# Every fourth expert's value row summed by the vector engine into SBUF instead of by TensorE

## The reference, cut to what matters

```
act = gelu(einsum('btd,bthkd->bthk', xi, u_tab[expert]))            # 8 heads x 16 experts for each token
ffn = einsum('bthk,bthkd->btd', gate * act, v_tab[expert])
x   = layer_norm(4 ** 0.25 * x + ffn, ln2_g, ln2_b)                 # x: 256 tokens x 1024
```

## Time and profile before

| | |
|---|---|
| time, median of 3 runs (lowest to highest) | 2979.73 us (2973.87 to 2981.59) |
| the profiled execution's own time | 2973.29 us |
| its span, first to last instruction | 2971.5 us |
| TensorE busy | 2618.1 us, 88% |
| VectorE busy | 1431.6 us, 48% |
| ScalarE busy | 916.0 us, 31% |
| GpSimd busy | 681.0 us, 23% |
| expert rows moved by DMA | 536.90 MB of 839.09 MB |
| first expert fetch issued, last expert matmul ended | 1175.57 us, 2960.93 us |
| shares of the chain that ended last | PE 61%, DVE 15%, DMA 14%, ACT 7% |

### The profile page before, as it was taken

How to read it: one execution, slowest core, us unless ns; L and a number is a source line. 1 busy time by engine, 2 the same in 40 slices (tenths; PEclk the granted TensorE clock), 3 DMA queues, 4 the chain that set the end, 5 groups by cost and what they waited for, 6 DMA issues and landing times.

```text
span 2971.5 us, 30335 instructions
## 1 busy us (share of the span) xinstructions
PE 2618.1 (88%) x11408; PEld 1774.3 (60%) x11408; DVE 1431.6 (48%) x3191; ACT 916.0 (31%) x2318; POOL 681.0 (23%) x615
## 2 busy tenths in 40 slices
PE   7776999878999995999998899999799999878776
PEld 6665888755884884766554566565376655443222
DVE  3776333242001234665546654545665554676444
ACT  1452111220000120354523235432334442333333
POOL 0010111110000001223233323333322333433432
PEclk9888999998999997999999999999899999999999
DMA  6220211214332665998999898999999899998997
GB/s 253 85 78 38 77 66 43 71 57 156 142 142 107 262 242 213 395 394 359 365 418 419 347 389 356 421 411 419 388 359 400 337 383 416 408 378 332 419 421 329
DMA packets 109986, 839.09 MB, mean 282 GB/s; under 512 B 12176, under 2 KB 12432, under 8 KB 13968
## 3 DMA queue, kind: packets, MB, share of 16 engines
q0 software_dynamic: 73728, 536.90, 44.8%
q1 hardware_dynamic: 36112, 300.25, 25.6%
HBM read 836.06 MB, written 1.05 MB: 282 GB/s over the span
## 4 chain that ended last, share of the span: by engine, by line
PE 61%; DVE 15%; DMA 14%; ACT 7%; issue 2%; POOL 1%; SPq 0%; POOLq 0%; DVEq 0%; ACTq 0%
PE psm L2129 17%; DMA mem<-in_puv,mem 14%; PE psm L427 10%; PE psm L1701 6%; PE psm L435 5%; DVE mem L2173 3%; PE psm L1348 3%; PE psm L716 3%; PE psm L2004 3%; PE psm L1245 3%; PE psm L1891 2%; PE psm L1396 1%; DVE mem L672 1%; PE psm L431 1%; PE psm L731 1%
## 5 line engine op out<-in xcount | busy, mean ns | idle before, releaser
L2129 PE MATMUL psm<-mem 128*128 128x512 f32 x2048 | 1017.5, 625 | 164.7 <-ACT mem L2147 160.8
L2173 DVE CUSTOM_DVE_ANT_0 mem<-mem 128x1024 f32<-128x1024 f32 x512 | 624.4, 1223 | 466.8 <-DMA mem<-in_puv,mem 463.0
L2157 POOL DMA_INDIRECT mem<-in_puv,mem x512 | 563.4, 1100 | 1205.4 <-PE psm L2129 1146.0
L2129 PEld LDWEIGHTS psm<-mem 128*128 128x128 f32 x2048 | 376.0, 196 | 607.8 <-ACT mem L2147 300.5
L427 PE MATMUL psm<-mem 128*128 128x256 f32 (+2 forms) x1504 | 355.1, 400 | 55.7 <-DVE mem L534 36.0
L427 PEld LDWEIGHTS psm<-mem 128*128 128x128 f32 x1504 | 294.5, 198 | 115.5 <-issue 52.7
L2141 ACT ACTIVATE mem<-mem 128x1 f32<-128x1 f32 x512 | 102.3, 200 | 692.0 <-DVE mem L2173 688.9
L1701 PE MATMUL psm<-mem 128*128 128x256 f32 x1024 | 243.7, 385 | 0.5 <-ACT mem L1424 0.5
L1701 PEld LDWEIGHTS psm<-mem 128*128 128x128 f32 x1024 | 196.2, 193 | 68.8 <-issue 45.0
L2147 ACT ACTIVATE mem<-mem 128x128 f32<-128x128 f32 x512 | 206.0, 402 | 17.0 <-PE psm L2129 0.3
L435 PE MATMUL psm<-mem 128*128 128x128 f32 x1408 | 191.2, 280 | 19.4 <-ACT mem L984 5.9
(11 more groups left out here) (356 smaller groups left out, 2413.6 us busy)
## 6 DMA issues: line engine op xcount, KB each, us to landing
mem<-in_w2g SPq DMA_DIRECT2D x64, 1024.0 KB
mem<-in_w SPq DMA_DIRECT2D x18, 2048.0 KB, 8.4
mem<-in_pwq SPq DMA_DIRECT2D x32, 1024.0 KB
mem<-in_w2f SPq DMA_DIRECT2D x28, 1024.0 KB
mem<-in_wgu SPq DMA_DIRECT2D x11, 2048.0 KB, 7.5
mem<-in_w2t SPq DMA_DIRECT2D x20, 1024.0 KB
mem<-in_w2b SPq DMA_DIRECT2D x16, 1024.0 KB
mem<-in_w2o SPq DMA_DIRECT2D x16, 1024.0 KB
```

What stands on the lines that cost most here:

```text
L2129: m = pe.matmul(bank(6 + h), DG[:, n % 4, :], GR[n % PING][:, 1024 + h * 512:1536 + h * 512], start=k == 0, stop=k == 127)
L2157: po.indirect_dma_start(GR[n % PING], None, A[f"puv{i // 2}"], bass.IndirectOffsetOnAxis(ap=IX[i % 2][:, k:k + 1], axis=0)).then_inc(gsem[ ...
L2173: ve.tensor_tensor_reduce(out=GR[n % PING][:, 0:1024], in0=GR[n % PING][:, 0:1024], in1=X[:, i % 2, :], scale=1.0, scalar=0.0, op0=MUL, op ...
```

## The change

The steps with n % 4 == 1 (32 of each tile, 128 in all) are summed by VectorE: `add_v(n)` runs behind the dot product of step n + 2, waits for `EA[n]`, and adds the coefficient times the v half to `ACC`, 1024 numbers for each partition in SBUF, with one `scalar_tensor_tensor` (the first of a tile overwrites `ACC` with a `tensor_scalar`). ScalarE makes no diagonal matrix and TensorE no matmuls for them. The buffer of such a step is freed by VectorE's mark `ED[n]`. The other 384 steps go as before. Behind the last of a tile, k = 125, VectorE also adds 4 ** 0.25 times x to `ACC`. `fin_ve` then adds `ACC` to the PSUM banks with `tensor_tensor` where it had `scalar_tensor_tensor` with x.

```diff
--- before.py
+++ after.py
@@ -221,6 +221,7 @@
         GT_ = [at(place(128), 128) for t in range(2)]
         DO = [at(place(128), 128) for t in range(2)]
         CO = [at(place(128), 128) for t in range(2)]
+        ACC = at(place(1024), 1024)
         assert placed[0] <= NF
         KY = at(5 * 2048, 16, 128)
         QP = at(scr, 16, 128)
@@ -400,9 +401,15 @@
         TP = marks("t_p", [(i, c) for i in RI for c in R4])
         TA = marks("t_a", [(i, c, x) for i in RI for c in R4 for x in ("s", "e")])
         TV = marks("t_v", [(i, c, x) for i in RI for c in R4 for x in ("ix", "g3", "gt")])
-        EP, EA, EV = [marks(n, range(NE)) for n in ("e_p", "e_a", "e_v")]
+        by_dve = [n for n in range(NE) if n % 4 == 1]
+        by_pe = [n for n in range(NE) if n % 4 != 1]
+        EP, ED = marks("e_p", by_pe), marks("e_d", by_dve)
+        EA, EV = marks("e_a", range(NE)), marks("e_v", range(NE))
+
+        def taken(n):
+            return EP[n] if n in EP.value else ED[n]
         PP = marks("p_p", [(i, c) for i in R2 for c in R2])
-        PV = marks("p_v", [(i, x) for i in RI for x in ["x0", "x1", "st", "l"] + ["h"] * (i < 2)])
+        PV = marks("p_v", [(i, x) for i in RI for x in ["ac", "x0", "x1", "st", "l"] + ["h"] * (i < 2)])
         PA = marks("p_a", R2)
         PO = marks("p_o", RI)
 
@@ -2117,6 +2124,7 @@
 
 
 
+
         def expert_pe(pe):
             yield
             yield
@@ -2124,10 +2132,12 @@
                 i, k = n // 128, n % 128
                 if k == 0 and i:
                     pe.wait_ge(*PV[i - 1, "x1"])
-                pe.wait_ge(*EA[n])
-                for h in R2:
-                    m = pe.matmul(bank(6 + h), DG[:, n % 4, :], GR[n % PING][:, 1024 + h * 512:1536 + h * 512], start=k == 0, stop=k == 127)
-                m.then_inc(EP.next(n), 1)
+                if n in EP.value:
+                    f = EP.value[n] % 4
+                    pe.wait_ge(*EA[n])
+                    for h in R2:
+                        m = pe.matmul(bank(6 + h), DG[:, f, :], GR[n % PING][:, 1024 + h * 512:1536 + h * 512], start=k == 0, stop=k == 127)
+                    m.then_inc(EP.next(n), 1)
                 yield
 
         def expert_ac(ac):
@@ -2140,11 +2150,14 @@
                 ac.wait_ge(*EV[n])
                 ac.activation(co, DO[i % 2][:, k:k + 1], ACT.Gelu).then_inc(oa.up(), 1)
                 ac.wait_ge(*oa.now())
-                ac.activation(co, co, ACT.Copy, scale=g).then_inc(oa.up(), 1)
-                ac.wait_ge(*oa.now())
-                if n >= 4:
-                    ac.wait_ge(*EP[n - 4])
-                ac.activation(DG[:, n % 4, :], ident, ACT.Copy, scale=co).then_inc(EA.next(n), 1)
+                e = ac.activation(co, co, ACT.Copy, scale=g)
+                if n in EP.value:
+                    e.then_inc(oa.up(), 1)
+                    ac.wait_ge(*oa.now())
+                    if EP.value[n] > 4:
+                        ac.wait_ge(*EP[EP.names[EP.value[n] - 5]])
+                    e = ac.activation(DG[:, EP.value[n] % 4, :], ident, ACT.Copy, scale=co)
+                e.then_inc(EA.next(n), 1)
                 yield
             yield
 
@@ -2153,7 +2166,7 @@
             if k % 32 == 0:
                 po.wait_ge(*TV[i, k // 32, "ix"])
             if n >= PING:
-                po.wait_ge(*EP[n - PING])
+                po.wait_ge(*taken(n - PING))
             po.indirect_dma_start(GR[n % PING], None, A[f"puv{i // 2}"], bass.IndirectOffsetOnAxis(ap=IX[i % 2][:, k:k + 1], axis=0)).then_inc(
                 gsem[n % PING], 16)
 
@@ -2172,9 +2185,27 @@
                 ve.wait_ge(gsem[n % PING], 16 * (n // PING + 1))
                 ve.tensor_tensor_reduce(out=GR[n % PING][:, 0:1024], in0=GR[n % PING][:, 0:1024], in1=X[:, i % 2, :], scale=1.0, scalar=0.0,
                                         op0=MUL, op1=ADD, accum_out=DO[i % 2][:, k:k + 1]).then_inc(EV.next(n), 1)
-                yield
-            yield
-            yield
+                add_v(ve, n - 2)
+                yield
+            yield
+            yield
+
+        def add_v(ve, n):
+            if n not in ED.value:
+                return
+            i, k = n // 128, n % 128
+            v, co = GR[n % PING][:, 1024:2048], CO[i % 2][:, k:k + 1]
+            ve.wait_ge(*EA[n])
+            if k == 1:
+                if i:
+                    ve.wait_ge(*PV[i - 1, "x1"])
+                ve.tensor_scalar(ACC, v, co, None, MUL).then_inc(ED.next(n), 1)
+            else:
+                ve.wait_ge(*ED[n - 4])
+                ve.scalar_tensor_tensor(ACC, v, co, ACC, MUL, ADD).then_inc(ED.next(n), 1)
+            if k == 125:
+                ve.wait_ge(*ED[n])
+                ve.scalar_tensor_tensor(ACC, X[:, i % 2, :], al, ACC, MUL, ADD).then_inc(PV.next((i, "ac")), 1)
 
 
         def fin_ve(ve, i):
@@ -2183,9 +2214,10 @@
             st, mv, v = ln_parts(t)
             x = X[:, t, :]
             ve.wait_ge(*EP[128 * i + 127])
+            ve.wait_ge(*PV[i, "ac"])
             for h in R2:
-                xx = x[:, h * 512:h * 512 + 512]
-                ve.scalar_tensor_tensor(xx, xx, al, bank(6 + h), MUL, ADD).then_inc(PV.next((i, f"x{h}")), 1)
+                c = slice(h * 512, h * 512 + 512)
+                ve.tensor_tensor(x[:, c], bank(6 + h), ACC[:, c], ADD).then_inc(PV.next((i, f"x{h}")), 1)
                 yield
             ve.wait_ge(*PV[i, "x1"])
             for k in R2:
```

## The result

The changed kernel takes 2988.81 us (median of 6 runs, 2984.45 to 2994.74) where the one before takes 2975.55 us (6 runs, 2972.71 to 2981.59). The ratio is 1.0052 with a 95% interval of 1.0039 to 1.0064: slower by some 15 us. 2972 us had been forecast, 0.31 had been given to slower by more than 0.3%, and the range of 2944 to 3012 us held the time.

What follows compares the result with a forecast made beforehand. DMA rate was taken as the bound, except eight stretches where TensorE's order binds. Terms -25 + 3 + 5 + 1 + 8 = -8 us gave a median of 2972 us; range 2944 to 3012 us.

Steps and rivals of the forecast that it cites:

- What bounds the kernel: Whole kernel: DMA at 421 GB/s bounds the tail and most else; TensorE's order binds only eight stretches between 1200 and 2725 us.
- TensorE's relief, 25 us: Eight TensorE-bound stretches: a quarter less expert work gains 25 us, 60% of at most 42; ends 0 and 42.
- the two long holes: Low-rate holes at 1825 and 2300 us, at a block without expert steps: they remain, about as wide.
- VectorE's time, 3 + 5 + 1 us: Added VectorE work: 3 us lost at 2600 to 2725 us, 5 at ends of tiles 0 to 2, 1 for x terms.
- the 1 for the x terms: Ends of tiles 0 to 2: the extra x term may delay normalisation, up to 1.24 us x 3, counted as 1.
- The release outside the tail, 8 us: Full stretches outside the tail: later buffer release costs 0.1 us for some 80 steps, 8 us lost; ends 0 and 50.
- The tail, 0 us: Tile 3's steps alone, 2750 to 2950 us: accumulations fit VectorE's idle time, 2.49 us a step stays, nothing lost.
- 0.7 us to spare: Margin for the fetch of n + 6 after the later release, with the fetch 1 us longer.
- Rival (c): VectorE steps where DMA is full, outside the eight stretches: four periods for release and fetch bind; +34 us, 3014 us; chance 0.27.
- The clock and the last part: Tail: clock-slowed steps, 2 us late, covered by 4.6 us margin, 0; tile 3's end: 3.08 us wait covers last VectorE work.

Runs made afterwards that it cites:

- the kernel with tiles 0 to 2: The changed kernel with VectorE summing every fourth step in tiles 0 to 2 only, tile 3 as before the change; 2967.40 us, ratio 0.9979 to the kernel before.
- the first experiment: The changed kernel with each accumulation one step earlier, behind the dot product of n + 1 (a tile's first excepted); 2974.83 us, ratio 1.0001 to the kernel before.

## Why the prediction was wrong, point by point

By its own terms the forecast put -11 us into tiles 0 to 2 (-25 + 5 + 1 + 8), +3 beside tile 3's selection and 0 into the tail and the end. The two profiles have -4.2, +3.6, +10.5 and +4.6, and -3.1 in the part that is not touched.

**What bounds the kernel: right.** The DMA rate bounds the tail and most of the rest, and TensorE the stretches of the earlier trace rows. The kernel with no accumulation shows it: nothing gained in the steps alone, 27.7 us beside other work.

**TensorE's relief, 25 us: right.** 27.7 us in the profile, 32 by the times; with a late release 24.8 and 22. That the two long holes remain was right too: 25 us from 1825 still stand at 246 GB/s, and of some 13 us without a transfer at 2300 us some 10 are left, though the DMA is fuller on both sides of them (323 GB/s for 266).

**VectorE's time, 3 + 5 + 1 us: the term for tiles 0 to 2 was too small.** Accumulations alone cost 15.4 us there in the profile where 5 stood in the sum (the 1 for the x terms is not in this experiment), and 6.5 beside tile 3's selection where 6.2 stood ahead of TensorE's saving; by the times it is 14 us for the whole kernel. I had charged only the tile ends and tile 3's selection, where VectorE is busy 83% and 75% of the time. Steps 112 to 128 cost 4.8 us in that profile, as forecast; the rest, steps 24 to 32 above all, was priced at nothing, and the mean busy share does not tell it. This and the release eat most of the relief: -27.7 + 15.4 + 3 to 10 is -9 to -2, and -4.2 was measured. By the times, -32 + 14 + 10 is -8 (tile 3's selection is in it), and the kernel with tiles 0 to 2 gave -6. With a scatter of some 8 us in tiles 0 to 2 the sum is no closer check than this.

**The release outside the tail, 8 us: right in size, as far as it can be told.** 3 to 10 us, for a number chosen between far ends.

**The tail, 0 us: the step that failed.** The working said 9.3 us of loop against 9.95 and kept "0.7 us to spare"; the charge was made "outside the tail" and the tail was left at zero because VectorE is half idle there. How busy VectorE is had nothing to do with it. The term that was mis-sized is the fetch: 5.77 us plus 1.0 for the longer fetch, 6.8, where 7.9 was measured. The 5.77 us had been read as a fetch into an idle queue; one earlier fetch was still on its way (used at 2115.30 us), and in the tail there are two. From the dot product to the fetch it is 2.7 us (2813.70 to 2816.40), together 10.6, and 72 steps, 18 rounds, took 190.9 us, 10.6 each. Before, they took 10.0 with a rare longer one. So the tail gives 10.5 us, the largest miss, and turns -8 into +2.5; the smaller gain in tiles 0 to 2 and the end make it the 11.2 of the profiles. Rival (c) had the mechanism and the point from which it decides, and had the place wrong: it was priced for the steps in which weights also flow, where it cost little, and it bound where nothing else fills the queue.

**The clock and the last part.** TensorE's gaps grew to 2.8 to 3.0 us, as forecast. The granted clock fell in the tail to 0.90, and to 0.88 in the first experiment, which runs at the full rate: in the tail the cover held, and 0 was right. The last accumulation and x term were covered too, since VectorE still waited 2.41 us for TensorE behind them. The last steps and the end took 4.6 us more all the same. 2.7 us of it are the loop: steps 505 to 511 took 17.6 us where they had taken 14.8. The rest is the clock, at the one place where nothing covers it. TensorE's last expert step, before and after:

```profile
2958.94 1.99 PE L2129 MATMUL psm<-mem 128*128 128x512 f32 x4 [0.45 <-ACT mem L2147]
2968.31 3.78 PE L2139 MATMUL psm<-mem 128*128 128x512 f32 x4 [1.61 <-ACT mem L2159]
```

Behind idle times of 2.94 and 1.61 us the granted clock was 0.50, the level of 1.2 GHz, where it had been 1.00, and the final sum waits for this step: 1.8 us that the forecast had at nothing.

**What stays open.** Why the loop's fetch takes 7.9 and not 6.8 us was not taken apart; it varies from 7.2 to 9.9 us. It depends on what else is on its way: in the kernel with the later accumulation in the tail, where the loop's fetch starts with one earlier fetch outstanding instead of two, the same 19 fetches took 6.3 to 6.9 us, 6.5 on average, lengthened as they were. And why eight well-placed steps a tile gain 19 us while 25 that include most of the same places gain 3 to 7 is explained only in its direction (each accumulation costs, most reliefs bring nothing).

## What to carry to other kernels

When a buffer's release is moved to another engine's in-order stream, write down what that release now waits for, and look whether the fetch that it permits is itself the thing waited for in the next round. If it is, the ring is as long as that loop, not as the number of buffers, and its fetch must be sized with as many transfers outstanding as there will be. Give work to a half-idle engine only for the steps in which the relieved engine is what the ring waits for; the rest of the steps pay for the engine's time and bring nothing.

## What the runs showed of the hardware

A fetch by GpSimd that starts early in a two-input VectorE instruction takes 1.8 to 2.0 us in place of 0.95. With over 0.5 us of the added instruction still to run, it took 1.64 us on average where that had two SBUF inputs (21 fetches) and 0.96 where it had one (23 fetches). In the tail of the changed kernel 16 of the 20 fetches of the loop took 1.81 us or more, since the release comes 0.1 us ahead of the next dot product. The mean over 512 fetches was 1100 ns in the kernel before, 1091 with the one-input instruction added, 1142 with two inputs and 1161 in the changed kernel. The Trainium skill ("SBUF — State Buffer", section "SBUF: two separate sides") gives the reason, a port pair that a VectorE instruction with two SBUF inputs and a GpSimd instruction that reads SBUF hold in turn. The runs agree with it on the length of the fetch, and show that the slowdown of 14 us was the same with one input.

The accumulation took 1281 ns on average where the same form took 1221 in the experiment that added it on other data; why is not known.
